# V projected for all head pairs before the first pair, with x stationary and its parts kept in DRAM; GpSimd takes the normalisation

## What is computed

```python
def reference(x, p, ...):                       # DEPTH = 1, the layer's mixer is neighborhood_attention
    mix = neighborhood_attention(x, na_w_qkv[0], na_rpb[0], na_w_o[0])
    x = layer_norm(ALPHA * x + mix, ln1_g, ln1_b)
    hid = square(relu(x @ w_ff1))
    ple = sigmoid(x @ w_ple_gate) * (p @ w_ple_proj)
    return layer_norm(ALPHA * x + hid @ w_ff2 + ple, ln2_g, ln2_b)

# neighborhood_attention: qkv = x @ w_qkv; 16 heads of 64; a 16 x 64 grid of tokens
#   s = q k^T / 8 + rpb over 8 rows x 16 columns of neighbours; out = softmax(s) v; out @ w_o
```

## Time and profile before

| | us |
|---|---|
| median of 3 runs (1225.02 to 1225.45) | 1225.35 |
| span of the profiled execution | 1223.4 |
| TensorE busy | 1213.5 (99%) |
| VectorE busy | 883.5 (72%) |
| ScalarE busy | 593.6 (49%) |
| GpSimd busy | 103.9 (8%) |

### The profile page before, as it was taken

How to read it: one execution, slowest core, us unless ns; L and a number is a source line. 1 busy time by engine, 2 the same in 40 slices (tenths; PEclk the granted TensorE clock), 3 DMA queues, 4 the chain that set the end, 5 groups by cost and what they waited for, 6 DMA issues and landing times.

```text
span 1223.4 us, 17911 instructions
## 1 busy us (share of the span) xinstructions
PE 1213.5 (99%) x5820; PEld 1020.1 (83%) x5820; DVE 883.5 (72%) x1744; ACT 593.6 (49%) x1144; POOL 103.9 (8%) x71
## 2 busy tenths in 40 slices
PE   9999999999999999999999999999999999999997
PEld 8888888888888888888888888888888888888886
DVE  3777677777777867769677777777764575588786
ACT  3555655655556843244444444444453433333671
POOL 0212222122123004200000000000000000000000
PEclk9999999999999999999999999999999999999999
DMA  8332223213233857683556566565579776768633
GB/s 219 83 76 71 58 72 89 55 55 75 55 107 84 274 158 233 209 286 118 192 207 240 177 221 218 184 239 178 220 239 379 280 274 223 258 238 309 192 104 103
DMA packets 162870, 215.61 MB, mean 176 GB/s; under 512 B 11504, under 2 KB 91504, under 8 KB 162416
## 3 DMA queue, kind: packets, MB, share of 16 engines
q1 hardware_dynamic: 162656, 214.59, 54.1%
q10 hardware_dynamic: 144, 0.13, 0.0%
HBM read 147.44 MB, written 58.90 MB: 169 GB/s over the span
## 4 chain that ended last, share of the span: by engine, by line
PE 98%; DMA 1%; DVE 0%; ACT 0%; issue 0%; DVEq 0%; SPq 0%; ACTq 0%
PE bank L2784 25%; PE bank L2752 25%; PE bank L1227 19%; PE bank L1378 7%; PE bank L2708 6%; PE bank L1333 4%; PE bank L1310 3%; PE bank L1289 3%; PE bank L1265 3%; PE bank L1371 1%; PE bank L1243 1%; PE bank L258 1%; PE bank L1281 1%; DMA ple_embedding<-bias_in 0%; DMA attention_T<-out_T 0%; DMA x_chunk<-in_x 0%
## 5 line engine op out<-in xcount | busy, mean ns | idle before, releaser
L887 ACT ACTIVATE probabilities<-negated_scores,negated_max 128x384 f32<-128x384 f32 (+1 forms) x128 | 75.7, 591 | 136.1 <-DVE negated_max L1103 135.7
L1227 PE MATMUL bank<-act_T_hi,w_qkv_hi 128*128 128x512 f32 x336 | 133.6, 398 | 0.0
L1227 PE MATMUL bank<-act_T_lo,w_qkv_hi 128*128 128x512 f32 x336 | 133.5, 397 | 0.0
L1227 PE MATMUL bank<-act_T_hi,w_qkv_lo 128*128 128x512 f32 x336 | 132.0, 393 | 0.0
L2752 PE MATMUL bank<-x_combination,weight_parts 128*128 128x512 f32 x504 | 118.5, 389 | 0.0
L1084 DVE TENSOR_TENSOR prob_T_lo<-bank,prob_T_hi 128x256 fp32r<-128x256 f32 (+2 forms) x160 | 69.1, 449 | 58.5 <-ACT prob_T_hi L878 56.8
L2752 PEld LDWEIGHTS bank<-x_combination,weight_parts 128*128 128x128 f32 x504 | 94.6, 188 | 19.6
L2752 PE MATMUL bank<-act_T_hi,weight_parts 128*128 128x512 f32 x240 | 77.3, 389 | 0.0
L2110 ACT ACTIVATE hidden_staging<-hidden_staging 128x512 f32<-128x512 f32 x48 | 30.4, 633 | 95.0 <-DVE hidden_staging L2450 95.0
L778 POOL TENSOR_TENSOR w_qkv_lo<-weight_raw,w_qkv_hi 128x1024 fp32r<-128x1024 f32 x21 | 50.3, 2396 | 294.5 <-ACT w_qkv_hi L833 294.5
L2784 PE MATMUL bank<-x_combination,hidden_parts_odd 128*128 128x512 f32 (+1 forms) x324 | 73.1, 381 | 0.0
(11 more groups left out here) (263 smaller groups left out, 2806.6 us busy)
## 6 DMA issues: line engine op xcount, KB each, us to landing
hidden_combinations<-hidden_staging SPq DMA_DIRECT2D x112, 256.0 KB, 2.6
w_ff_in<-in_w_ff SPq DMA_DIRECT2D x27, 1024.0 KB, 8.1
weight_raw<-in_w_ff SPq DMA_DIRECT2D x25, 1024.0 KB, 5.7
weight_raw<-hidden_combinations SPq DMA_DIRECT2D x14, 1024.0 KB, 5.5
hidden_in<-hidden_combinations SPq DMA_DIRECT2D x14, 1024.0 KB, 5.6
weight_raw<-in_na_w_qkv SPq DMA_DIRECT2D x21, 512.0 KB, 4.4
bias_in<-rpb_rows SPq DMA_DIRECT2D x256, 6.0 KB
attention_T<-out_T SPq DMA_DIRECT2D x8, 512.0 KB, 3.2
```

The lines of the kernel that those rows point to most:

```text
L887: nc.scalar.activation(prob[:, u % 4, 0:n], score[:, u % 2, 0:n], ACT.Exp, scale=-1.0, bias=nmax[:, u % 4:u % 4 + 1], accum_out=total[:, u ...
L1227: mm = nc.tensor.matmul(proj_ps[gi % 2][:, :], w[wp][:, (par + kind) % 2, k, :], S.act[ap][:, k, t * HALF:(t + 1) * HALF], start=(i == 0), ...
```

## The change

V of all eight pairs is projected in the first stage. The token chunk of x is now stationary and 512 columns of the V weights move, so V comes out with tokens on partitions and needs no transposes. There are 16 tiles (8 token tiles x 2 column halves) of 24 matmuls in eight banks in turn; six are started chunk by chunk as x arrives, the others follow whole. ScalarE and VectorE split each tile into parts (`v_high`, `v_low`) in four places, and SP stores it to `v_parts` in DRAM (512 KB). `load_v` brings one pair's parts back (1 MB) during the pair before. K and Q of pair 0 follow in one piece (`project(0, 0, 0, FILL)`).

The bodies fill with K and Q only: four groups, 96 matmuls, evacuated at steps 5, 10, 15 and 20 (before: K and Q at 10, 14, 17, 20). The weights have one place per kind. `normalise` loses its multiply to GpSimd: VectorE's `invert_total` makes the reciprocal, GpSimd multiplies with it broadcast. GpSimd makes the low parts of the weights in quarters (128 x 256) between the multiplies. In a body ScalarE copies Q's weights at step 1 and K's (of pair j+2) at step 12; before it was K at 1, Q at 9 and V at 18.

The diff, cut:

```diff
-FILL = 6 * GROUP_MMS
+PAIR_GROUPS = 4
+FILL = PAIR_GROUPS * GROUP_MMS
 FILL_STEPS = STEPS - 1
 
-EVAC_STEP = [(GROUP_MMS * (gi + 1) - 1) * FILL_STEPS // FILL + 1 for gi in range(6)]
-V_TURN_STEP = (4, 7)
+EVAC_STEP = [(GROUP_MMS * (gi + 1) - 1) * FILL_STEPS // FILL + 1 for gi in range(PAIR_GROUPS)]
...
+W_PIECES = 4
+Q_LOW_STEP = (2, 3, 4, 5)
+BIAS_STEP = (10, 17)
+K_LOW_STEP = (13, 14, 15, 16)
...
+            def store_v(n):
+                c, g = divmod(n, GROUPS)
+                row = 2 * 2 * HEAD
+                sp.wait_ge(v_lo, n + 1)
+                dst = bass.AP(S.v_parts, (c * (PAIRS // 2) * P * GROUPS + g) * row,
+                              [[GROUPS * row, P], [P * GROUPS * row, PAIRS // 2], [1, row]])
+                sp.dma_start(dst, v_place[n % V_PLACES][:, :, :, :].bitcast(F32)
+                             .rearrange("p (j h) a d -> p j (h a d)", h=2)).then_inc(v_stored[n % V_PLACES], 16)
...
+            def body(j, par, nth, more, loads):
+                if more:
+                    sp.wait_ge(pv_done, value(UNITS * j + 3))
+                    load_v(1 - par, j + 1)
                 if loads:
                     column = value(j * P + 2 * P)
-                    for kind in range(3):
-                        split = value(3 * j + (3 + kind + 1))
+                    for kind in (K_, Q_):
+                        split = value(split_count(kind, j + 1))
...
+            def normalise(j, u):
+                n = P * len(blocks_of(u % GROUPS))
+                pool.wait_ge(recip_done, UNITS * j + (u + 1))
+                nc.gpsimd.tensor_tensor(prob[:, u % 4, 0:n], prob[:, u % 4, 0:n],
+                                        recip[:, u % 4:u % 4 + 1].to_broadcast([P, n]), ALU.mult).then_inc(prob_ready, 1)
...
+                for s in range(UNITS + NORMAL):
+                    if s >= NORMAL:
+                        normalise(j, s - NORMAL)
+                    if more and s in Q_LOW_STEP:
+                        i = Q_LOW_STEP.index(s)
+                        split(Q_, j + 1, i, i + 1)
+                    if more and s in BIAS_STEP:
+                        h = BIAS_STEP.index(s)
+                        pool.wait_ge(score_done, UNITS * j + (GROUPS * (h + 1) + 2))
+                        build_bias(h, 16 * ROWS * j + 2 * 16 * ROWS)
+                    if loads and s in K_LOW_STEP:
+                        i = K_LOW_STEP.index(s)
+                        split(K_, j + 2, i, i + 1)
...
-            def normalise(j, u):
-                n = P * len(blocks_of(u % GROUPS))
+            def invert_total(j, u):
                 dve.wait_ge(exp_done, UNITS * j + (u + 1 + 2))
                 nc.vector.reciprocal(recip[:, u % 4:u % 4 + 1], total[:, u % 4:u % 4 + 1]).then_inc(recip_done, 1)
-                dve.wait_ge(recip_done, UNITS * j + (u + 1))
-                nc.vector.tensor_scalar(prob[:, u % 4, 0:n], prob[:, u % 4, 0:n], recip[:, u % 4:u % 4 + 1], None,
-                                        ALU.mult).then_inc(prob_ready, 1)
...
+            def v_products(n, k, passes=(0, 1, 2)):
+
+                c, g = divmod(n, GROUPS)
+                for i in passes:
+                    wp, ap = PASSES[i]
+                    mm = nc.tensor.matmul(v_bank(n), S.act[ap][:, k, g * P:(g + 1) * P], w_v[wp][c][:, k, :],
+                                          start=(k == 0 and i == 0), stop=(k == KC - 1 and i == 2), skip_group_check=True)
...
-            def turn_v(jn, t):
-                pe.wait_ge(proj_free, 6 * jn + (t + 1 + 2))
-                turn_v_half(t)
...
+            for n in range(FIRST_TILES, V_TILES):
+                v_tile(n)
+            pe.wait_ge(v_lo, GROUPS + 2)
+            project(0, 0, 0, FILL)
+            pe.wait_ge(v_lo, V_TILES)
```

More of the change, by code:

```diff
@@ L638, in _ @@
             sp.dma_start(col_mask[:, :], mask).then_inc(mask_loaded, 16)
+            for n in range(V_PLACES):
+                store_v(n)
+            for kind in (K_, Q_):
+                sp.wait_ge(w_lo, 2 * (kind + 1) + 2)
+                load_w(kind, 0)
+            for n in range(V_PLACES, GROUPS):
+                store_v(n)
             sp.wait_ge(ident_step, 3)
@@ L938, in _ @@
             act.sem_inc(exp_done, 2)
-            act.sem_inc(w_hi, 3)
             x_high(0, 0)
@@ L950, in _, with body @@
                 x_high(k, 1)
-                if k == 5:
-                    split(1, V_, 32, 3)
-            first_evac(K_, 0)
-            first_evac(K_, 1)
-            turned_v(0, 0, 0)
-            first_evac(Q_, 0)
-            turned_v(0, 0, 1)
-            first_evac(Q_, 1)
-            def body(j, par, more, loads):
+            for n in range(V_TILES):
+                v_high(n)
+                if n < KC // 2:
+                    second_split(2 * n)
+                    second_split(2 * n + 1)
+                if n == GROUPS:
+                    for kind in (K_, Q_):
+                        split(kind, 0)
+            for gi in range(PAIR_GROUPS):
+                evac(0, 0, gi)
+                if gi == 1:
+                    split(K_, 1)
+            for i in range(V_PLACES):
+                act.wait_ge(v_stored[i], V_STORED)
+            def body(j, par, nth, more, loads):
                 for s in range(STEPS + 1):
@@ L1135, in _ @@
                 x_low(k, 1)
-            for kind, t in FREED_ORDER:
-                first_evac(kind, t)
-            turned_v(0, 0, 0)
-            first_evac(Q_, 0)
-            turned_v(0, 0, 1)
-            first_evac(Q_, 1)
+            for n in range(V_TILES):
+                v_low(n)
+            for gi in range(PAIR_GROUPS):
+                evac(0, 0, gi)
             def early_low(t):
@@ L1405, in _ @@
             idle_products(WARM[1])
-            for n in range(3):
-                for t in range(2):
-                    for kind in FIRST_KINDS:
-                        first_products(kind, t, 0, (n,))
-                    if n == 1 and t == 0:
+            for i in range(3):
+                for n in range(FIRST_TILES):
+                    first_products(n, 0, (i,))
+                    if i == 1 and n == FIRST_TILES // 2 - 1:
                         for half in range(2):
@@ L1413, in _ @@
             for k in range(1, KC - TAIL):
-                for n, (t, kind) in enumerate((t, kind) for t in range(2) for kind in FIRST_KINDS):
+                for n in range(FIRST_TILES):
                     if n == 2:
@@ L1420, in _, with body @@
                             turn_x(k + 2, half)
[L1421 to L1422 removed]
+                    first_products(n, k)
+            for n in range(FIRST_TILES):
                 for k in range(KC - TAIL, KC):
[L1424 to L1428 removed]
+                    first_products(n, k)
+            for n in range(FIRST_TILES, V_TILES):
[3 more added lines that the diff above has]
+            pe.wait_ge(v_lo, V_TILES)
+            def body(j, par, nth, more, loads):
                 for s in range(STEPS):
```

363 lines of the change are left out of this document (162 added, 201 removed).

## The result

The changed kernel takes 1266.1 us, median of four runs (1264.7 to 1267.2), against 1225.2 us for the kernel before: ratio 1.0331, 95% interval 1.0318 to 1.0343. The forecast was 1256 us in a range of 1232 to 1268: slower, as forecast, and by 10 us more. The profiled execution has a span of 1263.7 us.

A forecast was written before the change was run, and what follows sets the result against it. TensorE, 99% busy, was taken as the bound. 1223.4 less 7.0 us of V transposes is 1216.4; 38.3 us of ring waits over seven pairs make 1254.7 of span, 1256.6 with 1.95 added; said 1256, range 1232 to 1268 us.

The forecast's parts named there:

- Ring: In each pair, bias add, exp, high copy, low part, next bias add: 2.20 us a turn, which sets the pair.
- Closing: From unit 15's bias add to the next pair's first: evacuation, reciprocal, GpSimd's multiply, then TensorE's work, 10.9 us.
- both GpSimd rows fit one line: Argument against GpSimd as bound: its 384-column add (1.01 us) and 1024-column low part (2.40 us) agree.
- Pair: Time from one pair to the next, 43.1 us, with TensorE waiting 5.6 us where it waited for nothing.
- V stage: First stage with V of all pairs: 336 more TensorE matmuls, evacuations and stores covered; 0, bounds -1 and +4 us.
- Last pair: Ten VectorE subtractions with two SBUF inputs beside 16 GpSimd multiplies, mostly hidden: 0, bounds 0 and +3 us.
- Shared port in the pairs: GpSimd's low part stretched VectorE's normalisation to 2.32 us; afterwards no such VectorE operation in the first seven pairs, so free.
- TensorE stays the bound: Rival: TensorE's lead carries the late part of a pair, pairs of at most 38.5 us, 1218 us; chance 0.12.
- The ring costs less: Rival: weight copy and evacuations hide in the pairs, 40.3 us each, 1238 us; no chance of its own given.
- GpSimd the bound: Rival: GpSimd's multiply takes 2.0 us, pairs of 47 us, 1285 us; chance 0.04.
- The statement on room: In the kernel before, a step took 2.36 us against a 2.20 us VectorE-ScalarE turn, so room is about nil.
- theory A: Follow-up theory: instructions are fetched in 256-instruction blocks; VectorE's loop starts four ahead of a block's end, so jumps fetch twice.

The follow-up runs named there:

- pad4: The changed kernel with four filler instructions (semaphore increments) on VectorE ahead of its loop: 1256.95 us, ratio 1.0257 to the kernel before.
- evac_split_last: evac_split with the multiply back on VectorE in the last pair alone: 1219.0 us, ratio 0.9948 to the kernel before.
- norm_vector: The changed kernel with four fillers and the multiply back on VectorE, GpSimd keeping the quarters: 1263.1 us, ratio 1.0304 to the kernel before.
- before_pad251: The kernel before with 251 fillers on VectorE in its first stage, so its loop stands against the blocks as the changed kernel's: 1232.7 us, ratio 1.0061.
- evac_split: The changed kernel with four fillers, VectorE's step reordered (reciprocal, bias add, low part), and K/Q evacuated one head per step except the last: 1220.3 us, ratio 0.9956.
- pad3: The changed kernel with three fillers instead of four on VectorE ahead of its loop: 1267.6 us (one run).

## Why the prediction was right, and where it was short

**The sum, against `pad4`,** which is the changed kernel without the fetches. Forecast of the span 1254.7 us, measured 1253.0 in the profiled execution, the fastest of four (the others 1254.7 to 1254.9); forecast of the time 1256, measured 1256.95. The mechanism is the one that the prediction named: in the pair from 254.91 us TensorE waits at the transposes of units 4, 9, 11, 12, 13 and 14, and the list had all of them but 13. That the sums agree so closely is in part luck, since errors of either sign cancel:

- *Ring.* Bias add of unit 0 to unit 4: 5.2 us said, 5.30 measured. The terms named for it do not add up to 5.2: three steps of 1.50 us and 1.6 us for exp, high copy and low part are over 6. What they leave out is that TensorE is ahead: in `pad4` the scores of the next pair's unit 1 start at 297.64 us, before the bias add of unit 0 at 297.99, and the bias adds of units 0 to 3 take 3.20 us instead of 4.5. Unit 4 to 15: 27.0 said, 27.28 measured, with the 2.20 us turn, 2.72 at an evacuation, 3.89 where output sum and K copy meet. The seventh pair, which has no K copy, needs 26.32: the 0.95 us less that the sum had for it.
- *Closing.* 10.9 said, 10.51 measured. Not quite half of the difference is GpSimd's multiply, put at 1.0 us and in fact 0.83 (0.61 for 256 columns). The quarter was estimated at 0.74 and takes 0.73. Against the 0.42 us of VectorE the multiply shows the factor of two that the Trainium skill gives for two-input operations ("GPSIMD Engine Reference", section 4.1). The forms differ, though: GpSimd's has two operands, VectorE's one and a scalar per partition (twice 0.42 is 0.84 us, where the prediction wrote 0.82). The argument that "both GpSimd rows fit one line" was empty, since two points always do.
- *Pair.* 43.1 said, 43.08 or 43.09 measured in each of the five pairs from the second to the sixth. The three parts were off by +0.10, +0.28 and -0.39 us: the agreement of the whole is better than that of its terms. The seventh interval, 51.3 us before, was put at some 44 us (51.3 - 12.0 + 5.6 - 0.95) and measured 43.05: its closing was 1.8 us longer than the others' before and is 0.9 us longer now (11.43 for 10.51). Why is not shown; TensorE's waits may hide the rest.
- *V stage.* Put at 0 us, it gained 1.4 (2.0 in `pad4`): the first bias add came at 126.43 us where 51.12 plus 336 matmuls of 0.231 less eight transposes make 127.9. From 60 us to the first bias add TensorE had no wait, and its 512-column matmuls stood just under 0.227 us apart, sixteen steps in the 3.62 us between these two. On 336 matmuls that is some 1.4 us:

```profile
80.27 0.39 PE L1270 MATMUL bank<-w_v_hi,act_T_lo 128*128 128x512 f32 x1
...
83.89 0.39 PE L1270 MATMUL bank<-w_v_lo,act_T_hi 128*128 128x512 f32 x1
```

  The same stage ended anywhere from 125.47 to 127.10 us in the nine traces of kernels that have it, so some tenths of this may be chance.

- *Last pair.* Put at 0, bounds 0 and 3 us: 1.4 us in `pad4`, 1.7 in the changed kernel. The cause that I gave, the shared port, is small. The ten subtractions with two SBUF inputs take 0.6 us more in `pad4` than in the kernel before: six of w_o's low parts 1.245 us each for 1.216, two of 896 columns 1.277 for 1.082, two more 1.254 for 1.220. In `evac_split_last`, with the multiply on VectorE, they are back at 1.216, 1.082 and 1.221 us, and the last pair is no shorter.
- *Shared port in the pairs.* No VectorE operation of the first seven pairs was to be of the blocked kind, and none is stretched; `norm_vector`, which puts one back, has it stretched at once.
- *The bound that is left.* "TensorE alone needs 37.5 us a pair" and "1218 us if TensorE stays the bound" were rivals' numbers; the version whose waits are gone has pairs of 37.77 us and takes 1219.0 us.

**The step that was missing** is the jump of the loop. The prediction counted which instructions VectorE issues and never where they stand. Two pairs of the seven took 4.1 and 4.2 us more than the others, and the two behind them 0.9 and 0.7 us more, at the lower clock: 9.8 us in all. By the medians `pad4` is 9.2 us faster, by the spans of the profiled executions 10.7. The profile of before could not show it, since it has 0.3 us at each jump: the place could have been counted, but its price of 3.0 and 2.1 us was in no row. So the range's upper end, set by longer pairs and by the last pair, held the result for another reason than it was made for. That the 1266.1 lies within it is luck; that `pad4`'s 1257 does is not.

**The rivals.** "TensorE stays the bound" was the right floor and the wrong order: it needed the bias add moved, and the evacuation split. "The ring costs less" (pairs of 40.3 us) and "GpSimd the bound" (47 us) did not occur; the pairs of 47 us that the trace has are VectorE's jumps.

**The statement on room** ("ring and TensorE run nearly level" before) held late in the pair, not at its start: in `before_pad251` a late VectorE won 2.7 us in the first four units and lost 0.6 in the next eleven.

## What to carry to other kernels

When a change shortens the engine that is the bound, write down the ring of the other engines with the durations of the trace, term by term: such a sum came within 0.1 us of a 43 us pair here (within 0.4 in each of its three parts), while the engines' busy shares (64% and less) said nothing. Then look for the one place in the ring where two operations can change order: no work was saved between 1257 us (`pad4`) and 1220 (`evac_split`), only the order changed and one operation was split. An order that pays in one kernel can cost in the next, since it cuts one ring and closes another, so it is tried on both. And a loop that is longer than one block of instructions can have a price that depends on where it stands in the instruction stream; when a kernel gets slower at its jumps, compare the time from branch to next instruction with the other engines', and move the loop by a few instructions before anything else.

## What the runs showed of the hardware

- VectorE's jump back cost 0.24 to 0.28 us when its loop (282, 314 or 330 instructions) began, by the count of theory A, at a block's start or one instruction behind it, and 2.7 to 3.1 us plus 2.1 us when it began one or four instructions ahead of one. One instruction more or less ahead of the loop decided over 10 us (`pad3`, `pad4`). The same jump of ScalarE, GpSimd and SP cost 0.3 us at most in both kernels.
- On the first pass through the same place nothing was lost: the first bias add (126.43 us) follows an evacuation that ends at 126.39. Running on in sequence, VectorE had the block in time.
- After a wait of 3.23 us TensorE's granted clock was 0.50 for about 3 us; so a pause of 4 us on another engine was paid for with 5. After the stop of 1.73 us in `before_pad251` (2.2 us for its weight load) it stayed at 1.00, as this window behind it shows:

```profile
158.00:161.00 3.00, 3.00 (x16) 1.00 0.48 178
```

- A multiply with one SBUF operand and a broadcast one took GpSimd 0.83 us for 384 columns, less than its add of two full operands of that size (1.01 us).
